# Two stages of a fused two-block kernel: low parts computed on VectorE, square sums issued two heads ahead, last sums added in PSUM, final weights split as their buffers come free

## The reference, cut to what matters

```python
o = rms_norm(o, norm_w) * jax.nn.silu(z)           # per head, over 128 channels
x = x + gate * (o.reshape(bsz, t, nh * dh) @ w_out)  # 2048 -> 1024
x = rms_norm(x, final_g)                           # end of block 1
h = _rmsnorm(x, norm_pre[l])                       # start of block 2
```

```python
ya = oa_normed * silu(za);  yb = hb_normed * silu(zb)
merged = sigmoid(ga) * (ya @ w_a) + sigmoid(gb) * (yb @ w_b)   # ga, gb = h @ parts of w_in
x = x + _rmsnorm(merged @ w_out, norm_post[l])
```

## Time and profile before

| | |
|---|---|
| median of 3 runs | 2483.99 us |
| the profiled execution, its own time | 2487.21 us |
| its span | 2485.4 us |
| busy PE / DVE / ACT / POOL | 2140.9 (86%) / 1197.3 (48%) / 850.7 (34%) / 492.6 (20%) us |
| stage_out | about 1056 to 1376 us of the span |
| stage_merge | about 2071 to 2485 us of the span |

### The profile page before, as it was taken

How to read it: one execution, slowest core, us unless ns; L and a number is a source line. 1 busy time by engine, 2 the same in 40 slices (tenths; PEclk the granted TensorE clock), 3 DMA queues, 4 the chain that set the end, 5 groups by cost and what they waited for, 6 DMA issues and landing times. The chain is left out here.

```text
span 2485.4 us, 29399 instructions
## 1 busy us (share of the span) xinstructions
PE 2140.9 (86%) x11304; PEld 1677.7 (67%) x11304; DVE 1197.3 (48%) x2121; ACT 850.7 (34%) x1348; POOL 492.6 (20%) x280
## 2 busy tenths in 40 slices
PE   3589999999999999567984789999899886999978
PEld 2467878787787878545763577666676655788767
DVE  5658677585958577345223433324223232522243
ACT  2365253435345352134112132433433442510121
POOL 0220202021110202034354221111111101432240
PEclk7789999999999999778997899999999998999989
DMA  6123232222323231164112211120211105211222
GB/s 272 36 73 99 61 101 90 69 88 69 94 63 104 65 101 48 41 236 147 45 35 80 76 56 34 51 77 26 79 50 34 60 26 195 85 51 43 76 85 85
DMA packets 126523, 199.22 MB, mean 80 GB/s; under 512 B 56324, under 2 KB 87812, under 8 KB 125232
## 3 DMA queue, kind: packets, MB, share of 16 engines
q1 hardware_dynamic: 126384, 197.34, 24.6%
HBM read 155.17 MB, written 42.11 MB: 79 GB/s over the span
## 5 line engine op out<-in xcount | busy, mean ns | idle before, releaser
L709 PE MATMUL p_job<-h_hi,w_hi 128*128 128x512 f32 x784 | 332.0, 424 | 45.9 <-DVE w_lo L850 23.1
L711 PE MATMUL p_job<-h_hi,w_lo 128*128 128x512 f32 x784 | 312.6, 399 | 0.0
L710 PE MATMUL p_job<-h_lo,w_hi 128*128 128x512 f32 x784 | 312.4, 398 | 0.0
L1691 PE MATMUL m_job<-h_hi,m_hi 128*128 128x512 f32 x592 | 262.0, 442 | 36.8 <-POOL m_lo L1527 36.8
L1693 PE MATMUL m_job<-h_hi,m_lo 128*128 128x512 f32 x592 | 238.4, 403 | 0.0
L1692 PE MATMUL m_job<-h_lo,m_hi 128*128 128x512 f32 x592 | 237.7, 402 | 0.0
L709 PEld LDWEIGHTS p_job<-h_hi,w_hi 128*128 128x128 f32 x784 | 151.6, 193 | 88.7 <-DVE w_lo L850 23.4
L1527 POOL TENSOR_TENSOR m_lo<-m_raw,m_hi 128x1024 fp32r<-128x1024 f32 x37 | 89.9, 2429 | 465.4 <-DVE m_hi L1799 465.4
L710 PEld LDWEIGHTS p_job<-h_lo,w_hi 128*128 128x128 f32 x784 | 151.7, 194 | 37.5 <-issue 8.2
L711 PEld LDWEIGHTS p_job<-h_hi,w_lo 128*128 128x128 f32 x784 | 151.2, 193 | 33.0
L1691 PEld LDWEIGHTS m_job<-h_hi,m_hi 128*128 128x128 f32 x592 | 115.3, 195 | 83.0 <-POOL m_lo L1527 37.5
(11 more groups left out here) (350 smaller groups left out, 4592.4 us busy)
## 6 DMA issues: line engine op xcount, KB each, us to landing
w_raw<-in_w SPq DMA_DIRECT2D x49, 512.0 KB, 3.6
m_raw<-in_w SPq DMA_DIRECT2D x37, 512.0 KB, 3.6
rows<-grows SPq DMA_DIRECT2D x32, 512.0 KB, 6.5
ada<-in_ada_w SPq DMA_DIRECT2D x8, 1536.0 KB, 12.5
e_raw<-in_w SPq DMA_DIRECT2D x24, 512.0 KB, 3.6
z_scr<-pre SPq DMA_DIRECT2D x16, 512.0 KB
o_scr<-oT SPq DMA_DIRECT2D x64, 128.0 KB, 1.8
ob<-o_scr SPq DMA_DIRECT2D x16, 512.0 KB, 4.2
```

The lines of the kernel that those rows point to most:

```text
L709: nc.tensor.matmul(p_job[h][:], hi, h_hi[:, k, cut], start=(k == 0), stop=False)
L710: nc.tensor.matmul(p_job[h][:], hi, h_lo[:, k, cut], start=False, stop=False)
L711: last = nc.tensor.matmul(p_job[h][:], lo, h_hi[:, k, cut], start=False, stop=(k == KD - 1))
L1691: nc.tensor.matmul(p_job[h][:], hi, h_hi[:, k, cut], start=(k == 0), stop=False)
```

## The change

In `stage_out`:
- GpSimd makes no `w_lo`, no `y_lo` and no square sums any more; VectorE does (`split`, the subtract of `y(1, n)`, `add_squares`). The cast of the head, `y(0, n)`, goes to ScalarE as a Copy. GpSimd keeps only the even `h_lo` chunks at the stage's end.
- VectorE's order for head n in pass 0 becomes: multiply by the inverse root, cast and subtract the weights of step n, subtract `y_lo`, and then the gate product of head n + 1.
- TensorE issues `sums(0)` and `sums(1)` at the start, and `sums(n + 2)` between the second and third chunk of step n.
- The adding of squares stops at chunk 5. Chunks 6 and 7 keep their squares in `sq` and `zb`, and TensorE adds three parts in PSUM (12 fp32 matmuls in place of 4).

In `stage_merge`:
- There is no GpSimd block; VectorE makes every low part. Its order for head n is y, cast, gate product of the next b head, `y_lo`, weights of job n + 2.
- `merged_hi(0..5)` is issued on ScalarE ahead of the gate of `gb` 7, with the low parts behind it on VectorE while job `("ab", 6)` runs. `wo_part(0..3)` waits only for the first half of the last job (`half_free`), and the low parts 0 to 3 stand on VectorE ahead of that job's products.

The core of the diff:

```diff
@@ stage_out, gpsimd @@
-                def add_squares(k):
...
-                    if q == 0:
-                        pool.wait_ge(yhi_done, n + 1)
-                        nc.gpsimd.tensor_tensor(y(1, n), zb[:, n % 3, :], y(0, n).bitcast(F32),
-                                                ALU.subtract).then_inc(ylo_done, 1)
-                    pool.wait_ge(whi_done, m + 1)
-                    nc.gpsimd.tensor_tensor(w_lo[:, m % 2, 0:cn], w_raw[:, m % 2, 0:cn],
-                                            w_hi[:, m % 2, 0:cn].bitcast(F32), ALU.subtract).then_inc(wlo_done, 1)
-                for k in range(first_ch[2], KD):
-                    add_squares(k)
@@ stage_out, scalar: squares(k), then the heads @@
+                        dst = total[:, r, :] if k == 0 else zb[:, r, :] if k == KD - 1 else sq[:, r, :]
...
+                square(0)
+                for n in range(V_HEADS):
+                    act.wait_ge(ss_done, n + 1)
                     if n >= 1:
+                        act.wait_ge(y_done, n)
...
+                    nc.scalar.activation(rinv[:], rinv[:], ACT.Exp, scale=-0.5).then_inc(rinv_done, 1)
+                    if n + 1 < V_HEADS:
+                        square(n + 1)
+                    act.wait_ge(y_done, n + 1)
+                    nc.scalar.activation(y(0, n), zb[:, n % 3, :], ACT.Copy).then_inc(yhi_done, 1)
@@ stage_out, tensor @@
                 sums(0)
+                sums(1)
                 for m, (q, n) in enumerate(steps):
-                    if q == 0 and n + 1 < V_HEADS:
-                        sums(n + 1)
                     pe.wait_ge(ylo_done, n + 1)
                     pe.wait_ge(wlo_done, m + 1)
                     for c in range(CH_PASS[q]):
+                        if q == 0 and c == 2 and n + 2 < V_HEADS:
+                            sums(n + 2)
...
+                for part in range(3):
+                    src = (total, sq, zb)[part]
+                    for r, bank in enumerate((p_ss, p_s2)):
+                        pe.wait_ge(added, 2 * (KD - 3) - 1 + r) if part == 0 else pe.wait_ge(
+                            sq2, 2 * (KD - 3 + part) + r + 1)
+                        for i in range(2):
+                            last = nc.tensor.matmul(bank[i][:], ones[:], src[:, r, i * HALF:(i + 1) * HALF],
+                                                    start=(part == 0), stop=(part == 2))
@@ stage_out, vector @@
+                gated(0)
                 for m, (q, n) in enumerate(steps):
-                    split_hi(m)
-                    if q and n == 0:
-                        drain(q - 1)
                     if q == 0:
...
                         nc.vector.tensor_tensor(z, z, rinv[:], ALU.mult).then_inc(y_done, 1)
-                        dve.wait_ge(y_done, n + 1)
-                        nc.vector.tensor_copy(y(0, n), z).then_inc(yhi_done, 1)
+                    split(m)
+                    if q == 0:
+                        dve.wait_ge(yhi_done, n + 1)
+                        nc.vector.tensor_tensor(y(1, n), z, y(0, n).bitcast(F32), ALU.subtract).then_inc(ylo_done, 1)
+                        if n + 1 < V_HEADS:
+                            gated(n + 1)
+                    elif n == 0:
+                        drain(q - 1)
+                    elif q == 2 and n % 2 and 1 <= n // 2 < first_ch[2]:
+                        add_squares(n // 2)
@@ stage_merge, scalar @@
+                    if c == KD - 1:
+                        act.wait_ge(job_done, LAST_GATE + 1)
+                        for k in range(KD - 2):
+                            merged_hi(k)
+                        act.wait_ge(m3, c)
                     gate(at[("gb", c)], sgb)
                 nc.scalar.preload_act_table_set(EXP_LN)
-                act.wait_ge(job_done, LAST_GATE + 1)
-                for k in range(KD - 1):
-                    merged_hi(k)
+                merged_hi(KD - 2)
+                act.wait_ge(half_free, 1)
+                for k in range(HA):
+                    wo_part(k)
                 act.wait_ge(job_done, NJ)
-                wo_part(0)
-                wo_part(1)
+                for k in range(HA, KD):
+                    wo_part(k)
                 merged_hi(KD - 1)
-                for k in range(2, KD):
-                    wo_part(k)
@@ stage_merge, vector @@
+                    if J == LAST_GATE:
+                        for k in range(KD - 2):
+                            merged_lo(k)
                     if what == "ab":
+                        if c == KD - 1:
+                            merged_lo(KD - 2)
+                            for k in range(HA):
+                                wo_low(k)
                         dve.wait_ge(job_done, J + 1)
...
+                for k in range(HA, KD):
+                    wo_low(k)
+                merged_lo(KD - 1)
```

More of the change, by code:

```diff
@@ L1158, in _, with square @@
                 nc.scalar.preload_act_table_set(EXP_LN)
[L1159 to L1164, removed]
-                    if n >= 1:
[L1166 to L1174, removed]
+                def square(n):
+                    act.wait_ge(oz_in[n % 3], 32 * (n // 3 + 1))
+                    if n >= 2:
+                        act.wait_ge(ss_done, n - 1)
+                    nc.scalar.activation(sq[:, n % 2, :], ob[:, n % 3, :], ACT.Square).then_inc(sq_done, 1)
+                square(0)
+                for n in range(V_HEADS):
+                    act.wait_ge(ss_done, n + 1)
+                    if n >= 1:
+                        act.wait_ge(y_done, n)
+                    for i in range(2):
+                        nc.scalar.activation(rinv[:, i * HALF:(i + 1) * HALF], p_ss[i][:], ACT.Ln,
+                                             scale=1.0 / DH, bias=eps[:, 0:1]).then_inc(ln_done, 1)
+                    act.wait_ge(ln_done, 2 * n + 2)
+                    nc.scalar.activation(rinv[:], rinv[:], ACT.Exp, scale=-0.5).then_inc(rinv_done, 1)
[3 more added lines that the diff above has]
+                    nc.scalar.activation(y(0, n), zb[:, n % 3, :], ACT.Copy).then_inc(yhi_done, 1)
                 for k in range(KD):
@@ L1225, in _ @@
                     last.then_inc(w_used, 1)
[L1227 to L1233, removed]
+                pe.wait_ge(ln_done, 2 * V_HEADS)
+                pe.wait_ge(bank_used, 2 * first_ch[2])
+                for part in range(3):
[3 more added lines that the diff above has]
+                            sq2, 2 * (KD - 3 + part) + r + 1)
+                        for i in range(2):
+                            last = nc.tensor.matmul(bank[i][:], ones[:], src[:, r, i * HALF:(i + 1) * HALF],
+                                                    start=(part == 0), stop=(part == 2))
+                        if part == 2:
+                            last.then_inc(ss2, 1)
                 pe.wait_ge(ri2, 1)
@@ L1259, in low, with add_squares, split @@
                                             ALU.subtract).then_inc(hlo[1], 1)
-                def split_hi(m):
+                def add_squares(k):
+                    for r in range(2):
+                        dve.wait_ge(sq2, 2 * k + r + 1)
+                        if k >= 2:
+                            dve.wait_ge(added, 2 * (k - 2) + r + 1)
+                        nc.vector.tensor_tensor(total[:, r, :], total[:, r, :], sq[:, r, :], ALU.add
+                                                ).then_inc(added, 1)
+                def split(m):
                     q = steps[m][0]
@@ L1300, in _ @@
                 dve.wait_ge(ms2, 4)
-                dve.wait_ge(ylo_done, V_HEADS)
                 for k in range(KD):
@@ L2193, in _ @@
                                                  k == 0, k == HA - 1)
+                            if q == 0 and J == NJ - 1:
+                                last.then_inc(half_free, 1)
                     else:
@@ L2243, in _, with split @@
             def _(dve):
-                def split_hi(J):
+                def split(J):
                     dve.wait_ge(w_in[J % 2], 16 * (J // 2 + 1))
@@ L2248, in split_hi, with merged_lo, wo_low @@
                     nc.vector.tensor_copy(w_hi[:, J % 2, :], w_raw[:, J % 2, :]).then_inc(w_hi_done, 1)
+                    dve.wait_ge(w_hi_done, J + 1)
+                    nc.vector.tensor_tensor(w_lo[:, J % 2, :], w_raw[:, J % 2, :], w_hi[:, J % 2, :].bitcast(F32),
+                                            ALU.subtract).then_inc(w_lo_done, 1)
+                def merged_lo(k):
+                    dve.wait_ge(mg_hi, k + 1)
+                    nc.vector.tensor_tensor(h_lo[:, k, :], mg[:, k, :], h_hi[:, k, :].bitcast(F32),
+                                            ALU.subtract).then_inc(mg_lo, 1)
+                def wo_low(k):
+                    dve.wait_ge(wo_hi, k + 1)
+                    nc.vector.tensor_tensor(y_lo[:, k, :], wo_raw[k], y_hi[:, k, :].bitcast(F32),
+                                            ALU.subtract).then_inc(wo_lo, 1)
                 def open_out(n):
```

(4 more changed lines are left out.)

89 lines of the change are left out of this document (26 added, 63 removed).

## The result

The changed kernel takes 2411.72 us in the median (2405.97 to 2416.63), the kernel before, beside it, 2484.68: a ratio of 0.970, with a 95% interval from 0.967 to 0.973. The prediction was 2411.0 in a range from 2402 to 2430.

The account below looks back on a forecast made before the run. TensorE, busy 86% of the span, was taken as the bound, with time to gain only at its standstills and slow clock. Terms summing to 74.2 us gave 2413.0 from the profiled 2487.2, or 2409.8 from the median; forecast 2411, range 2402 to 2430.

Parts of the forecast that it names:

- Pass 0: First pass of stage_out: TensorE sets the pace at 5.86 us per head, so 94.5 us, 31.6 less.
- both rings: Pass 0's two dependency loops, through the Square and through y_lo: 5.5 us per head each, 0.36 below TensorE's 5.86.
- First matmul: Start of pass 0 in stage_out: the first matmul comes 2.0 us earlier, an estimate.
- pass 1: Second pass of stage_out: gains 0.3 us at its first weights, behind the drain.
- Pass 2: Third pass of stage_out: waits and most slow clock go, 45.9 us for 58.8, 12.9 less.
- Last sums: After pass 2 in stage_out: twelve fp32 matmuls start at once, 10.5 us for 15.2, 4.7 less.
- Behind the last job: stage_merge, last job to end of row tile 0: TensorE starts at once, 12.9 us for 30.2, 17.3 less.
- the stage's start: stage_merge: first low part 1.1 us earlier, third job 2.8 earlier, slow clock 1.5 less; 5.4 us together.
- The slower ring: Rival, chance 0.14: a ring in pass 0 is slower than TensorE; at 6.7 us per head 2423, up to 7.3 2431.
- The slow clock: Rival, chance 0.05: the slow clock stays when waits go; without its 16 us the gain is 58, giving 2429 us.
- The late final split: Rival, chance 0.06: in stage_merge merged casts or late weight loads slip, first tile takes 17 us; 2416 to 2420.
- Slower than before: Rival, chance 0.02: VectorE's wide operations stay at 3.4 us with GpSimd idle, pass 0 grows by 53; near 2520 us.

Follow-up runs that it names:

- a2_changed: The changed kernel itself, unaltered, run and profiled again later; 2411.03 us, ratio 0.971 to the kernel before.
- e4: The changed kernel with the weights' low parts in stage_out made by GpSimd again; 2411.14 us, ratio 0.970.
- e11: The changed kernel with VectorE's old order in pass 0 and the sums one head ahead; 2413.62 us, ratio 0.970.
- e9: The kernel before with sums two heads ahead and VectorE's new order in pass 0, GpSimd still making the low parts; 2483.37 us, ratio 0.998.
- e10: The changed kernel with GpSimd making both low parts in pass 0 again, and the weights' in all passes; 2425.08 us, ratio 0.976.
- e3: The changed kernel with the sums one head ahead again, all else as changed; 2414.70 us, ratio 0.971.
- e6: The kernel before with the sums two heads ahead, engines and their order unchanged; 2477.58 us, ratio 0.9965.
- e5: The changed kernel with the low part of the 16 heads made by GpSimd again; 2421.07 us, ratio 0.974.

## Why the prediction was right, point by point

**The sum.** Predicted 74.2 us; 70.6 in the first profile, 75.8 in the second (from the spans). In the changed code alone it is 74.6 and 75.6: in the first profile stage_mix took 6.2 us more and the work ahead of the first sums 2.2 less, by chance. Part of the hit is luck. By the same points stage_out gained 54.6 (second profile 54.5) for 51.5, and stage_merge 20.0 (21.1) for 22.7, so two misses of some 3 and 2 to 3 us cancel. The terms, from the first profile:

- Pass 0: -33.6 for -31.6. The pace of 5.86 per head was met (5.85), so both rings with 0.36 us to spare held. The start cost some 2.3 of the 4.3 us that I kept: this is the largest miss of stage_out.
- First matmul earlier by 2.9 for 2.0; pass 1 -0.5 for -0.3.
- Pass 2: -12.8 for -12.9. The additions on VectorE made nobody wait.
- Last sums: -4.7 for -4.7. Six groups start 1.72 apart:

```profile
1283.23 1.88 PE L1218 MATMUL p_ss<-zb,ones 128*128 128x512 f32 x4
1284.95 1.88 PE L1218 MATMUL p_out<-zb,ones 128*128 128x512 f32 x4
1286.93 1.26 ACT L1163 ACTIVATE rinv<-p_ss,eps 128x512 f32<-128x512 f32 x2 [4.84 <-PE p_out L1218]
```

- Behind the last job: 14.8 us from its last matmul's start to tile 1's, for 32.0, so -17.2 for -17.3. TensorE goes on at once and has one wait to speak of, for part 7; the waits for the residual's two inputs are 1.0 together, for 0.7:

```profile
2310.57 0.39 PE L2219 MATMUL e_b<-y_hi,h_hi 128*128 128x512 f32 x1
...
2320.60 0.47 PE L2219 MATMUL e_b<-y_hi,h_hi 128*128 128x512 f32 x1 [0.22 <-DVE h_lo L2242]
...
2322.58 1.09 PE L2202 MATMUL e_b<-ident,ab 128*128 128x128 f32 x8 [0.35 <-DMA ab<-x_scr]
2324.30 1.09 PE L2202 MATMUL e_b<-ident,ab 128*128 128x128 f32 x8 [0.63 <-DMA ab<-x_scr]
```

**The mis-sized term: the jobs of stage_merge.** I had -5.4 for the stage's start, 1.1 ahead of its first matmul and 4.3 within the jobs. a2_changed bears the 4.3 out: from the first job's first matmul to the third's it is 27.8 us for 30.9, to the last's 269.9 for 274.5, a gain of 4.6. (In the first profile it is 3.0: there the third job waited 1.3 us, and the cast ahead of it 1.2 for a load.) But the last job then took 11.9 us for 10.3, in both profiles, which left 3.0 and 1.4:

```profile
2297.97 0.70 PE L2160 MATMUL e_b<-y_hi,e_hi 128*128 128x512 f32 x1 [2.67 <-DVE g L2301]
2298.47 0.63 PE L2161 MATMUL e_b<-y_lo,e_hi 128*128 128x512 f32 x1
```

It stands behind a wait of 2.67 us that the kernel before has as well. There the granted clock stayed at 1.00 behind the wait; here it was 0.73 over the next 6.3 us. I had looked for the slow clock only where it was already in the trace. The other profiles have the same wait, 2.67 us. The clock fell behind it in eight of the ten kernels with the changed stage_merge, but not in e4 and e11, and in none of the four with the old one. So it goes with the changed stage in most profiles but not in all, and the reason stays open.

**Right in size, wrong in its reason.** The prediction says that TensorE, "only one head ahead with its sums, runs dry every second head", by a long chain that is slowed on both engines. The runs give the 33.5 us of pass 0 step by step: look-ahead and VectorE's order 3.5 (to e9), the head's cast and ScalarE's order 17.2 (to e10), the low parts' move off GpSimd 12.8. In the other direction look-ahead is worth 4.4 (e3). So one head ahead was not the main cause. The collision of GpSimd and VectorE is shown in the rows (3.36 for 1.28), but its price is not: e10 has almost none of it and still pays 12.8 for GpSimd's longer subtracts, so what the collision costs lies within the 17.2. I had read ScalarE's waits for loads only as a danger for the new order; in the kernel before they delayed nothing, and with the look-ahead alone (e6, e9) they held Ln back. The sum was unaffected, since it was built on TensorE's own pace and asked only whether every ring fits below it. My expectations for e5, e6, e9 and e10, which needed the size of a single cause, missed by 3 to 11 us.

**The rivals.** The slower ring: pitch 5.85, no. The slow clock: every stretch where I let it go shows 0.99 or 1.00, against the 58 us that this rival leaves of the gain. The clock's 16 us are a fifth of this gain. The Trainium skill, "TensorE: Matmul & The Clock Gate", section "What's actually happening", puts the ramp's cost at under 1% of a typical span. This case's trace doesn't agree: over the kernel before the clock is at 1.2 GHz for 335 of 2485 us, with TensorE busy in 178 of them, which is some 89 us or 3.6% by an estimate (half of the busy time). And the 16 us, left out, would have given 2429 for the measured 2411.7. The late final split: tile 0 took 11.7 us, not 17. Slower than before: VectorE's wide operations take 1.22 to 1.28 in pass 0.

## What to carry to other kernels

To predict a rebuilt loop, take the bound engine's own pace as its time and check each ring against it; how the old loop lost its time then mattered little here, while single causes, which didn't add up, were hard to size. Look for instructions with two durations in the trace (1.28 and 3.36 in the earlier trace rows): here they showed two engines that block each other, which the waits charged to somebody else. But don't put the whole gain down to it: a slower engine in the ring also costs by its own durations, as e10 shows. And look at what stands in an engine's queue behind an operation that waits for a load. The 56.8 us of ScalarE's idle time ahead of a Square cost nothing in the kernel before, and became a limit for the Ln behind it as soon as the sums came earlier.

## What I had not expected of the hardware

- Who starts first pays nothing: beside each other, a GpSimd subtract takes 2.4 and the gate product 3.4 us, or the gate product 1.28 and the subtract 3.13, by 0.1 to 0.4 us of order. Three that overlap took 4.4 us (e9, 1126.58 to 1130.94) for the 4.7 of their sum.
- The 384-wide subtract took 0.56 us on VectorE and 1.00 on GpSimd alone, and in e4 it cost the pass only 0.8.
- The granted clock over the 6.3 us behind the same wait of 2.67 us was 1.00 in the kernel before and 0.73 in the changed one, and 1.00 again in e4 and e11, whose stage_merge is the changed one; this stays open.
